# The gated-delta scan of a two-block layer: the backward direction's tokens move to the other half of the partitions

## What is computed

```python
def step(S, inp):                       # per head, S is 64 x 64
    r_t, w_t, kk_t, b_t, v_t, k_t = inp
    sa = jnp.einsum("bhvk,bhk->bhv", S, kk_t)
    S = (S * w_t[:, :, None, :] - sa[..., None] * b_t[:, :, None, :]
         + v_t[..., None] * k_t[:, :, None, :])
    return S, jnp.einsum("bhvk,bhk->bhv", S, r_t)
for d in range(2):                      # d == 1 runs reversed; the context's state comes first
    state, y = wkv_scan(init[d], rh, decay, kk, kk * a, vh, k_d, reverse=(d == 1))
    y_sum = y if y_sum is None else y_sum + y
```

## Time and profile before

| what | value |
|---|---|
| median of 3 runs | 2367.61 us (2366.77 to 2368.23) |
| the profiled execution, its own time | 2367.12 us |
| its span in the profile | 2365.3 us |
| TensorE busy, matmuls | 2165.8 us (92%) |
| VectorE busy | 1547.4 us (65%) |
| mean granted TensorE clock | 0.963 of 2.4 GHz |
| the scan | from about 485 to 851 us of the span |

### The profile page before, as it was taken

One profiled execution on the slowest core, in us unless ns is written; L12 is line 12 of the kernel. 1 busy time (PEld: TensorE's weight loads), 2 busy tenths in 40 slices (PEclk: granted clock), 3 DMA queues, 4 the chain that ended last, 5 costly groups with the idle time before them and its releaser, 6 DMA issues. The chain is left out here.

```text
span 2365.3 us, 42734 instructions
## 1 busy us (share of the span) xinstructions
PE 2165.8 (92%) x18008; PEld 1709.4 (72%) x18008; DVE 1547.4 (65%) x1999; ACT 865.3 (37%) x1371; POOL 780.9 (33%) x461
## 2 busy tenths in 40 slices
PE   7779999938899999899999998999899999999898
PEld 1657777638898977678888776887677767777666
DVE  5878658686677434878888885056455665645654
ACT  3443443403232253733333333145424443333321
POOL 0324433300000314487777763444322111111111
PEclk9889999968999999999999999999999999999899
DMA  7553343476655541212222237343122011101522
GB/s 278 194 186 127 102 131 127 140 203 160 164 139 135 130 148 54 79 69 80 81 80 80 80 114 255 125 153 118 48 99 80 36 54 63 54 27 45 196 71 81
DMA packets 250942, 271.45 MB, mean 115 GB/s; under 512 B 157176, under 2 KB 188536, under 8 KB 246400
## 3 DMA queue, kind: packets, MB, share of 16 engines
q1 hardware_dynamic: 246144, 251.94, 33.0%
q10 hardware_dynamic: 4608, 16.78, 2.0%
HBM read 200.48 MB, written 68.19 MB: 114 GB/s over the span
## 5 line engine op out<-in xcount | busy, mean ns | idle before, releaser
L105 PE MATMUL b_ps<-h_hi,b_wpool 128*128 128x512 f32 (+1 forms) x976 | 301.6, 387 | 20.7 <-issue 7.3
L2903 PE MATMUL g_ps<-g_h_hi,w 128*128 128x512 f32 x784 | 259.2, 402 | 5.3 <-ACT g_q L3096 5.3
L3216 POOL TENSOR_TENSOR w<-raw_down,w 128x1024 fp32r<-128x1024 f32 x38 | 93.9, 2472 | 461.6 <-ACT w L3074 461.6
L105 PEld LDWEIGHTS b_ps<-h_hi,b_wpool 128*128 128x128 f32 x976 | 183.4, 193 | 69.7 <-issue 19.6
L2172 DVE SCALAR_TENSOR_TENSOR e_vars<-grid,vec,e_vars 128x1024 f32<-128x1024 f32 x168 | 216.0, 1285 | 7.3 <-ACT e_vars L1919 4.2
L105 PE MATMUL b_ps<-h_lo,b_wpool 128*128 128x512 f32 (+1 forms) x488 | 185.1, 379 | 0.0
L2903 PEld LDWEIGHTS g_ps<-g_h_hi,w 128*128 128x128 f32 x784 | 148.5, 189 | 39.7 <-ACT g_q L3096 6.0
L2903 PE MATMUL g_ps<-g_h_lo,w 128*128 128x512 f32 x392 | 155.3, 396 | 0.0
L2584 POOL TENSOR_TENSOR g_down_lo<-raw_down,g_down_hi 128x1408 fp32r<-128x1408 f32 x26 | 86.8, 3345 | 140.4 <-ACT g_down_hi L2484 140.4
L2423 PE MATMUL g_pb<-g_z_hi,g_down_hi 128*128 128x512 f32 x286 | 115.0, 402 | 14.7 <-DVE g_down_lo L2661 9.8
L714 POOL TENSOR_TENSOR b_wpool<-raw_in,b_wpool 128x1024 fp32r<-128x1024 f32 x26 | 66.6, 2560 | 167.3 <-ACT b_wpool L512 167.3
(11 more groups left out here) (513 smaller groups left out, 5796.3 us busy)
## 6 DMA issues: line engine op xcount, KB each, us to landing
e_raw_up<-w_ffn SPq DMA_DIRECT2D x22, 1024.0 KB, 4.8
raw_down<-w_down SPq DMA_DIRECT2D x32, 704.0 KB, 4.2
c_op<-ops SPq DMA_DIRECT2D x40, 512.0 KB, 4.2
raw_down<-w SPq DMA_DIRECT2D x38, 512.0 KB, 3.5
b_xin<-ada_rows ACTq DMA_DIRECT2D x32, 512.0 KB, 5.3
ops<-b_xin SPq DMA_DIRECT2D x16, 1024.0 KB, 4.0
raw_in<-w SPq DMA_DIRECT2D x26, 512.0 KB, 4.0
zs<-e_z SPq DMA_DIRECT2D x21, 512.0 KB, 2.6
```

Of the source, the lines that this page charges most:

```text
L105: last = nc.tensor.matmul(out, w[:, k, :], x[:, k, cols], start=(k == 0 and n == 0), stop=(k == nk - 1 and n == 2))
L2903: mm = nc.tensor.matmul(out_bank, ww[w % 2][:, k], xx[g][:, k], start=(k == 0 and a == 0), stop=(k == KD - 1 and a == 2))
L3216: nc.gpsimd.tensor_tensor(w_lo[w % 2], raw[:, w % 2], w_hi[w % 2].bitcast(F32), ALU.subtract).then_inc(sem("lo"), 1)
```

## The change

The backward direction's token-major tensors exchange their halves: head h of x = 1 has its tokens on partitions ROWS[1 - h] (`h ^ x` in the code), while its channel-major tensors (`op`, `sc`) stay where they are. A product of x = 1 between tokens and channels so uses the two off-diagonal quarters of the array. The TensorE functions take both directions at once: they wait for both, interleave forward and backward product by product, and signal both at the end. The backward sum in `chain_g` and `chain_y` would mix quarters with one output, so its product of state and `op`, which stays in the diagonal quarters, goes first, with a semaphore of its own. `vc` of x = 1 is loaded in two transfers of 64 partitions in place of one of 128.

```diff
+        LOADED = (32, 48)
...
-                sp.dma_start(vc[x][u % 3][:], d["vts"][slot]).then_inc(S(f"loaded{u % 3}_", x), 16)
+                if x == 0:
+                    sp.dma_start(vc[x][u % 3][:], d["vts"][slot]).then_inc(S(f"loaded{u % 3}_", x), 16)
+                else:
+                    for h in HEADS:
+                        sp.dma_start(vc[x][u % 3][ROWS[1 - h]], d["vts"][slot, ROWS[h]]).then_inc(S(f"loaded{u % 3}_", x), 16)
...
-                                         raw[x][i % 2][quarter(h, b), :, :, cols32(b)].rearrange("p j q c -> p (j q) c")
+                                         raw[x][i % 2][quarter(h ^ x, b), :, :, cols32(b)].rearrange("p j q c -> p (j q) c")
...
-            def triangles(x, u, a):
-                if a == 0:
-                    wait("yd", x, u)
-                else:
-                    wait("bk", x, u + 1)
-                src = op[x][u % 3]
-                heads(quad(bank[x][a]), (src[:, B + a], src[:, R:B].rearrange("p a q c -> p q a c"))
-                      ).then_inc(S(("p_l", "p_m")[a], x), 1)
+            def triangles(u, a):
+                for x in DIRS:
+                    if a == 0:
+                        wait("yd", x, u)
+                    else:
+                        wait("bk", x, u + 1)
+                mm = [None, None]
+                for q in range(PAIRS):
+                    for x in DIRS:
+                        for h in HEADS:
+                            mm[x] = MM(quad(bank[x][a])[ROWS[h ^ x], q], op[x][u % 3][ROWS[h], B + a, q], op[x][u % 3][ROWS[h], R:B, q],
+                                       start=True, stop=True)
+                signal(("p_l", "p_m")[a], mm)
...
+            def summed(early, turn, out0, pairs0, out1, early1, pairs1):
+
                 for q in range(PAIRS):
                     for h in HEADS:
+                        last = MM(out1[ROWS[h], q], early1[0][ROWS[h], q], early1[1][ROWS[h], q], start=(q == 0), stop=False)
+                last.then_inc(sem(early), 1)
+                forward = [(q, n) for q in range(PAIRS) for n in range(len(pairs0))]
+                backward = [(q, n) for q in range(PAIRS) for n in range(len(pairs1))]
+                mm = [None, None]
+                for i, (q, n) in enumerate(forward):
+                    still, moving = pairs0[n]
+                    for h in HEADS:
+                        mm[0] = MM(out0[ROWS[h], q], still[ROWS[h], q], moving[ROWS[h], q], start=(n == 0), stop=(n == len(pairs0) - 1))
+                    if i == PAIRS:
+                        pe.wait_ge(sem(early), turn)
+                    if i >= PAIRS:
+                        q, n = backward[i - PAIRS]
+                        still, moving = pairs1[n]
+                        for h in HEADS:
+                            mm[1] = MM(out1[ROWS[h], q], still[ROWS[1 - h], q], moving[ROWS[1 - h], q], start=False,
+                                       stop=((q, n) == backward[-1]))
+                return mm
...
-            def chain_z(x, s):
-                wait("u", x, s + 1)
-                wait("gg", x, s + 1)
-                heads(half(bank[x][2], 1), (ud[x][s // 2 % 2][:, place(x, s)], gg[x])).then_inc(S("p_z", x), 1)
+            def chain_z(s):
+                for x in DIRS:
+                    wait("u", x, s + 1)
+                    wait("gg", x, s + 1)
+                mm = [None, None]
                 for q in range(PAIRS):
+                    for x in DIRS:
+                        for h in HEADS:
+                            mm[x] = MM(half(bank[x][2], 1)[ROWS[h ^ x], q], ud[x][s // 2 % 2][ROWS[h], place(x, s), q], gg[x][ROWS[h], q],
+                                       start=True, stop=True)
+                signal("p_z", mm)
```

More of the change, by code:

```diff
@@ L1176, in _ @@
         def _(pe):
[L1177 to L1184, removed]
             def wait(name, x, value):
@@ L1188, in wait, with signal @@
                     pe.wait_ge(S(name, x), value)
[L1190 to L1195, removed]
+            def signal(name, last):
+                for x in DIRS:
+                    last[x].then_inc(S(name, x), 1)
+            MM = nc.tensor.matmul
@@ L1196, in blocks @@
+            def blocks(i):
+                for x in DIRS:
+                    wait(f"pre{i % 2}_", x, 16 * (i // 2))
+                    wait("raw", x, i - 2)
+                out = [bank[x][3][:].rearrange("p (j q c) -> p j q c", j=2, q=PAIRS) for x in DIRS]
+                mm = [None, None]
                 for j in range(2):
                     at = slice(C * j, C * j + C)
-                    mm = heads(out[:, j], (src[:, still, :, at], src[:, moving, :, at]))
-                mm.then_inc(S("p_pre", x), 1)
@@ L1205, in token_major @@
+                signal("p_pre", mm)
+            def token_major(u):
+                for x in DIRS:
+                    wait(f"loaded{u % 3}_", x, (u // 3 + 1) * LOADED[x])
+                    wait("mt", x, u)
+                out = [bank[x][1][:].rearrange("p (a q c) -> p a q c", a=2, q=PAIRS) for x in DIRS]
+                mm = [None, None]
                 for a in range(2):
                     for q in range(PAIRS):
-                        for rows in ROWS:
-                            mm = nc.tensor.matmul(out[rows, a, q], op[x][u % 3][rows, B + a, q], t["c_ident"][rows, rows],
-                                                  start=True, stop=True)
@@ new lines, in level_y @@
+            def level_y(u):
+                for x in DIRS:
+                    wait("lt", x, u + 1)
+                    wait(f"inv{u // 2 % 2}_", x, 96 * (u // 4 + 1))
+                mm = [None, None]
+                for q in range(PAIRS):
+                    for x in DIRS:
+                        for h in HEADS:
+                            at = quarter(h ^ x, x)
+                            mm[x] = MM(first(bank[x][0])[quarter(h, 1 - x), q], lt[x][u % 2][at, q, 1, cols32(1 - x)],
+                                       td[x][u // 2 % 2][at, place(x, u), q, cols32(x)], start=True, stop=True)
+                signal("p_yd", mm)
@@ new lines, in last_u @@
+            def last_u(u):
+                for x in DIRS:
+                    wait("yd", x, u + 1)
+                mm = [None, None]
+                for q in range(PAIRS):
+                    for x in DIRS:
+                        for h in HEADS:
+                            at = quarter(h, 1 - x)
+                            mm[x] = MM(first(bank[x][3])[quarter(h, x), q], yd[x][at, q],
+                                       ud[x][u // 2 % 2][at, place(x, u), q, cols32(1 - x)], start=True, stop=True)
+                signal("p_u", mm)
@@ L1233, in last_u @@
-            def last_u(x, u):
-                wait("yd", x, u + 1)
-                j = place(x, u)
-                for q in range(PAIRS):
[L1237 to L1247, removed]
@@ new lines, in summed, with chain_g @@
+                return mm
+            def chain_g(s):
+                for x in DIRS:
+                    wait("mt", x, s + 1)
+                    wait("sc", x, s + 1)
+                    wait("yo", x, s - NCTX)
+                of_v, of_s = ([(mt[x][s % 2][:, :, 1], vc[x][s % 3]) for x in DIRS], [(op[x][s % 3][:, KK], sc[x][s % 2]) for x in DIRS])
+                signal("p_g", summed("early_g", s + 1, half(bank[0][2]), (of_v[0], of_s[0]), half(bank[1][2]), of_s[1], (of_v[1],)))
+            def chain_z(s):
+                for x in DIRS:
+                    wait("u", x, s + 1)
+                    wait("gg", x, s + 1)
+                mm = [None, None]
+                for q in range(PAIRS):
+                    for x in DIRS:
+                        for h in HEADS:
+                            mm[x] = MM(half(bank[x][2], 1)[ROWS[h ^ x], q], ud[x][s // 2 % 2][ROWS[h], place(x, s), q], gg[x][ROWS[h], q],
+                                       start=True, stop=True)
+                signal("p_z", mm)
@@ new lines, in chain_s @@
+            def chain_s(s):
+                for x in DIRS:
+                    wait("zc", x, s + 1)
+                mm = [None, None]
+                for q in range(PAIRS):
+                    for n in range(2):
+                        for x in DIRS:
+                            still, moving = bk[x][s % 2][:, 1 - n], (vc[x][s % 3], zc[x])[n]
+                            for h in HEADS:
+                                at = ROWS[h ^ x]
+                                mm[x] = MM(half(bank[x][2])[ROWS[h], q], still[at, q], moving[at, q], start=(n == 0), stop=(n == 1))
+                signal("p_s", mm)
@@ new lines, in chain_y @@
+            def chain_y(s):
+                for x in DIRS:
+                    wait("s1", x, s + 1)
+                of_s, of_v, of_z = ([(sc[x][s % 2], op[x][s % 3][:, R]) for x in DIRS], [(vc[x][s % 3], mt[x][s % 2][:, :, 0]) for x in DIRS],
+                                    [(zc[x], lt[x][s % 2][:, :, 0]) for x in DIRS])
```

(30 more changed lines are left out.)

39 lines of the change are left out of this document (13 added, 26 removed).

## The result

The changed kernel takes 2378.62 us (median of 8 runs, 2374.71 to 2384.84) against 2368.49 for the kernel before beside it (8 runs, 2361.95 to 2376.37). The ratio is **1.0043**, 95% interval 1.0027 to 1.0060: slower by 0.43%, where 2347 and faster was forecast. A later comparison gave 1.0040 (1.0027 to 1.0053), 2372.98 us against 2365.76.

A forecast was written before the change was run, and what follows sets the result against it. TensorE was taken to bound the late scan, SyncE's load queue the earlier steps. Steps 0 to 11 net -2.0 us and step 12 to the end -18 sum to -20, from 2367.1 to 2347 us; range 2322 to 2363.

The forecast's parts named there:

- So the quarters' own occupancy is the limit, not issue: TensorE's products: a quarter is held 53 ns per 64 columns, so four quarters would give 15 ns a record, not 29.
- the step of 9.75 us: A late scan step after the change, joint waits included, against 14.2 us before; TensorE's work alone 7.85 us.
- x12 and x24: Records in `level_y` read as starting in 0.12 us: 12 with x = 0 alone, 24 with x = 1, 5 ns each.
- `triangles` of both directions in 0.9 us: Sign of being right: in 58 ns, records of four products start where two did; staying at 1.75 us meant wrong.
- The joint waits: Both directions end together and the next function waits for both copies, making a step 9.75 us, not 7.85.
- Rival (1): The four quarters do not run at once; joint waits cost 6.4 us and extra transfers 12 x 0.3: 2377, slower; chance 0.07.
- Extra transfers +3.6: SyncE's queue before step 12: 12 more issues at 0.3 us each, bounds 0 and 0.43, adding 3.6 us.
- Steps 0 to 11: Start to step 5 gain 0, held by SyncE's queue; steps 6 to 11 lose its 5.6 us wait; net -2.0 us.
- Rival (4): SyncE's queue is less rigid: first 12 steps gain 1 us each, late stalls vanish, 2323 us; chance 0.15.
- 92 us: Scan from step 12's `gg` to its end, against 110.2 before, a gain of 18 us.
- Rival (2): Late steps stay bound by loads, 13 us each; the end gains 7, extra issues take 4: 2364 us; chance 0.1.
- Rival (3): TensorE, idle more often, is granted 1.2 GHz after stalls in steps 12 to 15: 2353 us; chance 0.15.

The follow-up runs named there:

- joint_only: The changed kernel's order, joint waits and joint signals, but on the earlier partitions (two diagonal quarters), `vc` in one transfer; 2380.58 us, 1.0072 of the kernel before.
- changed_again: The changed kernel run once more, unaltered, as yardstick for two later runs; 2372.98 us against 2365.76 for the kernel before, 1.0040.
- split_vc: The kernel before, with only the backward `vc` loaded in two transfers of 64 partitions; 2369.24 us against 2366.88, 1.0014.
- halves_only: The changed kernel's partitions and `vc` transfers, but TensorE takes one direction after the other and signals each for itself; 2363.65 us, 0.9995 of the kernel before.
- y_small_products: The changed kernel, `chain_y` with 32 by 32 outputs in place of 64 by 64, as many instructions; 2373.66 us, 1.0034 of the kernel before.
- y_half_products: The changed kernel, `chain_y` for two of four pairs of heads, 96 instructions a step fewer; 2361.90 us, 0.9983 of the kernel before.
- double_instructions: The kernel before, each product of `heads` cut into two of half the moving columns, 384 products a step instead of 224; 2545.91 us, one run.

## Why the prediction was wrong

- **The step that failed** is "So the quarters' own occupancy is the limit, not issue", and with it the step of 9.75 us. 53 ns per 64 columns and 29 ns a record were read rightly, and the array can indeed do twice that. But an unstalled step before has some 904 TensorE records in 14.2 us, 4.0 us for each 256, and the supply brings 256 in 4.1 us in the median: nothing was left between the pace of before and the supply's. Even at the closest spacing, 3.4 us, the 3.5 blocks of a step are 3.5 x 3.4 = 11.9 us; my 9.75 lay below that. What I named as rival was that the quarters would not run at once; the trace shows them at once, and the stops besides.
- **A misreading of the earlier trace rows** that changed nothing: x12 and x24 count the records that run in a stretch, not those that start in it. 10 and 12 start, 16 ns apart for one direction and 8 where both run. So the 5 ns that the prediction sets against a least distance of 25 ns are 8 ns; that is still below it, and so are the 15 ns of `chain_z`.
- "`triangles` of both directions in 0.9 us": right, where no stop falls into it.
- **The joint waits**: their mechanism was right, their price too small. Rival (1) put them at 0.8 us in eight steps, 6.4 us; joint_only, without the extra transfers, is 13.7 us above before by the medians (1.0053 to 1.0091). 15 us of waits on `c_s` and `c_yd` stand in its trace, from 535 on.
- Extra transfers +3.6: right as far as 1.0014 (1.0002 to 1.0026) can tell. For the range I counted their bounds, 0 and 0.43 us each, as +-2 us; they are -3.6 and +1.6 about the 3.6.
- Steps 0 to 11: step 2's and step 6's `gg` were to stay within 4 us and came 5.5 and 6.7 us later. The 5.6 us wait of SyncE was to vanish; L1099 is L1104 now, and its waits on compute from 480 to 870 are, first after, then before:

```profile
SPq L1063 <- PE c_ps L1275: 17.9, 5, 10.1
SPq L1063 <- DMA tb<-c_ti: 13.5, 4, 4.5
SPq L1104 <- ACT c_raw L1365: 7.0, 2, 4.3
```

```profile
SPq L1062 <- PE c_ps L1182: 19.8, 7, 10.8
```

  The wait on `c_raw` stays, 7.0 us now in two pieces. Rival (4), a queue that eases, is not seen either. And the queue stands for `chain_y` to free a buffer as long as it did before (17.9 and 19.8 us), a row that I had left out when I called the queue unbroken and the 5.6 us its only long wait on compute; the longest of these is 10.8 us. A TensorE that is no faster holds the queue up as much. The start, which I put at 0, has a joint wait too: the first product follows the scan's first load by 8.8 us, against 5.4 before, since `token_major(0)` now waits for the loads of both directions (8.8 in joint_only and 7.7 in changed_again, but 5.3 in split_vc and halves_only).
- Step 12 to the end: "92 us" was forecast, 859.9 - 746.2 = 113.7 came, against 110.2. Steps 16 to 19 are 14.5, 16.3, 14.1 and 12.4 us apart, not 9 to 11: the last sign of being wrong, over 12. Rival (2), late steps bound by loads, is not it: after 710 us no product of the scan waits over 1 us for `vc`.
- Rival (3), the clock: it fell, to 0.945 over the span. But from step 16's `gg` to step 17's and on to step 18's the granted clock of the changed kernel was 1.00, and these took 16.28 and 14.05 us with 9.90 and 9.51 us of busy time:

```profile
807.84:824.12 16.28, 9.90 (x459) 8.96 (x453) 4.93 (x10) 3.92 (x12) 0.00 (x0) 1.00 0.57 118
824.12:838.17 14.05, 9.51 (x453) 8.67 (x443) 4.89 (x10) 3.92 (x12) 1.88 (x2) 1.00 0.36 95
```

  And joint_only is slower than the changed kernel (1.0072 against 1.0043 and 1.0040; the intervals just meet), and its granted clock from 535 to 850 is as high as before's. The stretch in before, then in joint_only:

```profile
535.00:850.00 315.00, 286.71 (x8667) 279.34 (x8663) 196.31 (x284) 93.89 (x258) 26.90 (x18) 0.96 0.56 137
```

```profile
535.00:850.00 315.00, 269.07 (x8275) 260.56 (x8277) 191.31 (x278) 83.98 (x254) 26.86 (x18) 0.97 0.57 138
```

  What a lower clock costs the changed kernel in its other stretches was not measured by itself.

**The sum as the runs have it**, in per cent: joint waits +0.72, extra transfers +0.14, four quarters the rest to +0.43, so -0.43 (give or take 0.3, by the three intervals): 10 us of gain, where I had TensorE's work shrink by 5.85 us in each of 20 steps and its busy time did shrink by some 3.9 in a late one. That the three add is assumed: by halves_only the quarters with the extra transfers but without joint waits give -0.05, so some -0.2 for the partitions alone.

That instruction blocks cause the stops rests on where they fall in the count of instructions, on y_small_products and on y_half_products. The last gains 11 to 13.5 us for 16 steps x 96 / 256 = 6 blocks, 1.9 to 2.2 us a block, less than 4.1, so not every block is on the path. Late steps take 14.9 us: 3.5 blocks at 4.1 us are 14.4, and the joint waits may be the rest. Why a block isn't fetched earlier I can't say. A form with fewer, larger products was not tried: stacking two products' contraction rows would need second copies written by VectorE.

## What to carry to other kernels

Before tiling small products over more of TensorE's array, count its instructions: a float32 product is four, 256 make a block, and here a block took 4.1 us in the median where TensorE waited for each, 16 ns an instruction, and never less than 3.3 us, 13 ns, however many quarters worked. If the kernel is near 16 ns an instruction already, as this one was, expect help from fewer instructions only, and a joint wait that the tiling brings is pure loss. In a profile the sign is idle time "issue" of 1 to 2 us in the middle of a function, with a packet of the queue of kind "instruction" that ended just before, and a multiple of 256 instructions from one such stop to the next.

## What the hardware showed that I had not expected

- The four 64 by 64 quarters of the array run at once, though each shares its rows with one and its columns with another: 15 ns a record of 64 columns against 29 with two.
- Halving the moving columns from 64 to 32 changed nothing in the time of a record in two quarters (double_instructions: 15.4 ns an instruction; 14.6 before).
- TensorE's instruction blocks are 16,384 bytes, mostly 0.9 to 1.5 us each in transfer, and never start closer than 3.3 us in nine traces of the scan. TensorE stops exactly at the head of a block that has not come (213 of 233 distances between such stops are 256 times the packets between), and goes on 1.1 to 1.7 us after the packet's end.
